# Down projection on one Trainium2 core: the sample rows' weight tiles taken in three turns instead of six in the first half of d_model

## What is computed

```python
def swiglu(h, w_gate, w_up, w_down):
    return (jax.nn.silu(h @ w_gate) * (h @ w_up)) @ w_down
...
        yp = yp + swiglu(rms_norm(yp, g_ffn[l]), w_gate[l], w_up[l], w_down[l])
        ys = ys + swiglu(rms_norm(ys, g_ffn[l]), w_gate[l], w_up[l], w_down[l])
```

## Time and profile before

| | before |
|---|---|
| median of three runs | 1028.95 us |
| the profiled execution | 1032.31 us |
| its span, first to last instruction | 1030.6 us |
| mean granted TensorE clock | 0.999 |
| TensorE busy | 1006.1 us, 98% of the span |
| VectorE, ScalarE, GpSimd busy | 61%, 38%, 40% |
| line 1482 (sample's tiles) | 88 records, 818.8 to 955.2 us |

### The profile page before, as it was taken

How to read it: one execution, slowest core, us unless ns; L and a number is a source line. 1 busy time by engine, 2 the same in 40 slices (tenths; PEclk the granted TensorE clock), 3 DMA queues, 4 the chain that set the end, 5 groups by cost and what they waited for, 6 DMA issues and landing times.

```text
span 1030.6 us, 16280 instructions
## 1 busy us (share of the span) xinstructions
PE 1006.1 (98%) x5754; PEld 836.8 (81%) x5754; DVE 625.8 (61%) x877; ACT 389.1 (38%) x701; POOL 408.4 (40%) x444
## 2 busy tenths in 40 slices
PE   5999999999999999999999999999999999999997
PEld 4999998888887787787787787877878776877786
DVE  5476637766245696676667567666754737634725
ACT  5411235445233443333333334333333446334431
POOL 2001100000000367697696787876964400201045
PEclk9999999999999999999999999999999999999999
DMA  8311331100321444553643643644637999578814
GB/s 277 96 51 43 84 85 43 43 2 1 123 103 67 148 113 130 160 165 109 190 151 113 193 144 112 201 135 134 184 110 227 296 335 385 188 281 310 308 41 169
DMA packets 166274, 155.84 MB, mean 151 GB/s; under 512 B 16240, under 2 KB 129296, under 8 KB 166224
## 3 DMA queue, kind: packets, MB, share of 16 engines
q1 hardware_dynamic: 166224, 155.16, 46.8%
HBM read 114.17 MB, written 41.06 MB: 151 GB/s over the span
## 4 chain that ended last, share of the span: by engine, by line
PE 84%; DMA 7%; DVE 4%; SPq 1%; issue 1%; ACT 1%; POOL 1%; POOLq 0%; ACTq 0%; DVEq 0%
PE ps L1108 26%; PE ps L1110 25%; PE ps L1109 25%; DMA xd_in<-act_scratch 2%; PE ps L1394 2%; PE ps L1145 1%; PE ps L1280 1%; DMA act_scratch<-act_sums 1%; DMA y_acc_odd<-in_w_down 1%; PE ps L1258 1%; DMA out_state_gmlp_v_sample<-work 1%; DMA act_scratch<-ffn_blocks_odd 1%; PE ps L1482 1%; PE ps L1242 1%; DMA act_scratch<-ffn_blocks_even 1%
## 5 line engine op out<-in xcount | busy, mean ns | idle before, releaser
L1108 PE MATMUL ps<-x_forms,w_forms 128*128 128x512 f32 (+1 forms) x644 | 246.4, 383 | 2.0 <-DVE w_forms L1903 1.7
L1109 PE MATMUL ps<-x_forms,w_forms 128*128 128x512 f32 (+1 forms) x644 | 244.7, 380 | 0.0
L1110 PE MATMUL ps<-x_forms,w_forms 128*128 128x512 f32 (+1 forms) x644 | 244.5, 380 | 0.0
L1108 PEld LDWEIGHTS ps<-x_forms,w_forms 128*128 128x128 f32 x644 | 121.0, 188 | 29.9 <-issue 4.8
L1110 PEld LDWEIGHTS ps<-x_forms,w_forms 128*128 128x128 f32 x644 | 121.1, 188 | 23.0
L1109 PEld LDWEIGHTS ps<-x_forms,w_forms 128*128 128x128 f32 x644 | 121.1, 188 | 22.4
L1108 PE MATMUL ps<-w_dn,x_dn 128*128 128x512 f32 x308 | 121.5, 394 | 0.0
L1110 PE MATMUL ps<-w_dn,x_dn 128*128 128x512 f32 x308 | 120.0, 390 | 0.0
L1109 PE MATMUL ps<-w_dn,x_dn 128*128 128x512 f32 x308 | 119.9, 389 | 0.0
L955 POOL TENSOR_SCALAR meansq<-sumsq 128x1 f32<-128x1 f32 (+1 forms) x26 | 9.8, 376 | 249.2 <-ACT xn_ffn L1530 224.1
L1689 ACT CAST w_forms<-w_sums 128x512 fp32r<-128x512 f32 x88 | 54.6, 623 | 111.1 <-PE ps L1110 108.7
(11 more groups left out here) (254 smaller groups left out, 2113.2 us busy)
## 6 DMA issues: line engine op xcount, KB each, us to landing
xd_in<-act_scratch SPq DMA_DIRECT2D x35, 512.0 KB, 7.3
t_raw<-in_w_down SPq DMA_DIRECT2D x88, 128.0 KB, 2.5
act_scratch<-act_sums SPq DMA_DIRECT2D x22, 512.0 KB, 4.1
y_acc_odd<-in_w_down SPq DMA_DIRECT2D x22, 512.0 KB, 6.3
wd_in<-t_scratch SPq DMA_DIRECT2D x20, 512.0 KB, 6.9
wd_in<-in_w_down SPq DMA_DIRECT2D x15, 512.0 KB, 6.7
stage<-in_w_in SPq DMA_DIRECT2D x28, 256.0 KB, 3.6
w_stage_even<-in_w_gate SPq DMA_DIRECT2D x22, 256.0 KB, 3.3
```

The lines of the kernel that those rows point to most:

```text
L1108: mm(out, wh, xh, start=first, stop=False, skip_group_check=onto)
L1109: mm(out, wh, xl, start=False, stop=False, skip_group_check=onto)
L1110: return mm(out, wl, xh, start=False, stop=last, skip_group_check=onto)
```

## The change

The six turns of the first half, with 2, 2, 2, 2, 2 and 1 tiles, become three with 4, 4 and 3. The loads of tiles 6 and 7 are issued two groups earlier in the queue. Tiles 8, 9 and 10, which were issued ahead of k = 14 (two) and k = 16 (one), are issued together ahead of k = 13. The second half is as it was.

```diff
-SAMPLE_TURNS = {(0, 3): 2, (0, 5): 2, (1, 1): 2, (1, 2): 2, (1, 3): 2, (1, 4): 1,
+SAMPLE_TURNS = {(0, 5): 4, (1, 2): 4, (1, 4): 3,
                 (3, 0): 2, (3, 2): 2, (3, 4): 2, (4, 0): 2, (4, 2): 2, (4, 3): 1}
 EARLY_SLOTS, LATE_SLOTS = 4, 2
 
-RAW_LOADS = {(1, 2): range(4, 6), (1, 5): range(6, 8), (2, 2): range(8, 10), (2, 4): range(10, 11),
+RAW_LOADS = {(1, 2): range(4, 6), (1, 3): range(6, 8), (2, 1): range(8, 11),
              (3, 5): range(11, 13), (4, 1): range(13, 15), (4, 3): range(15, 17), (5, 0): range(17, 19),
              (5, 2): range(19, 21), (5, 4): range(21, 22)}
```

## The result

| | before | changed |
|---|---|---|
| median | 1028.70 us (6 runs, 1027.25 to 1030.61) | 1033.08 us (6 runs, 1032.45 to 1033.86) |
| ratio | | 1.0034, 95% interval 1.0023 to 1.0045 |
| profiled execution, span | 1032.31, 1030.6 us | 1032.97, 1031.3 us |
| mean granted TensorE clock | 0.999 | 0.995 |

By the ratio the changed kernel is slower by 0.34%, 3.5 us with 2.4 to 4.6 as its interval; the two medians of the table are 4.4 us apart, inside that interval. The forecast was no change (1028.8 us), and its range ended at 1030.9. The granted clock was 0.995 in all six timed runs as well.

The account below looks back on a forecast made before the run. TensorE's chain and a full DMA queue were taken as bounds, meeting at row tile 3 of group 12. TensorE's 9.88 - 6.84 = 3.04 us gain mostly became a 2.9 us wait: 1028.95 - 0.1 = 1028.8 us, range 1026.6 to 1030.9.

Parts of the forecast that it names:

- The cost of a turn: On TensorE, a turn of two tiles costs 1.20 us, one of three or four tiles 2.08 us.
- the sum: On TensorE, 9.88 us removed less 6.84 added: 3.04 us early after turn (1, 4), of which 0.1 us is left.
- The removed waits: TensorE's waits for tiles at turns (1, 3) and (1, 4), 2.56 and 0.12 us, go.
- The new wait for x8: TensorE reaches group 8 earlier and waits 0.6 us for the low part of x8.
- The gain goes into a wait for the adds at row tile 3 of group 12: TensorE arrives there at 867.90 and waits 2.9 us for VectorE's sample adds, ending at 870.76.
- "The same bytes stand ahead of x16 in both kernels, so if the DMA queue never runs dry, x16 lands where it did": In the DMA queue, x16 isn't delayed by the reordered loads; its cast starts again near 865.7 us.
- The third rival: The DMA queue runs dry while SP stands at tiles 8 to 10; x16 lands late, 1030.9 us; chance 0.10.
- "[...] by the rows, 1028.8, since the gap is still shorter than the one that was followed by a fall": At row tile 3, a 2.9 us wait keeps TensorE's clock full; the fall seen followed more than 3.4 us idle.
- The price of a fall: A clock fall at row tile 3's wait would cost about 1.6 us, from 3.5 us at half clock.
- the second rival: TensorE's clock falls to half in the new wait at row tile 3: 1028.8 + 1.6 = 1030.4 us; chance 0.10.

Follow-up runs that it names:

- tile_3_later: Changed kernel with row tile 3 of group 12 moved on TensorE behind row tile 2 of group 13; 1027.89 us, ratio 0.9976 to the kernel before.
- adds_earlier_2: Changed kernel with VectorE's four sample adds moved ahead of the low parts of groups 15 and 16; 1027.07 us, ratio 0.9977 to the kernel before.
- after_look_2: Second profile of the changed kernel, without an edit; span 1031.8 us.
- loads_later: Changed kernel with tiles 6 and 7 issued ahead of group 10 instead of group 9; 1031.50 us, ratio 1.0016 to the kernel before.
- turns_alone: Kernel before with the new three turns (SAMPLE_TURNS) and the old RAW_LOADS; 1031.32 us, ratio 1.0015 to the kernel before.
- loads_alone: Kernel before with the old six turns (SAMPLE_TURNS) and the new RAW_LOADS; 1030.67 us, ratio 1.0011 to the kernel before.
- adds_later_1: Kernel before with VectorE's four sample adds moved behind the low parts of group 17; 1031.27 us, ratio 1.0009 to the kernel before.

## Why the prediction was wrong

- **The cost of a turn** (1.20 and 2.08 us): right, 2.06 measured, and 1.1 us for merging in the profiles where the sum has 0.96.
- **The removed waits** (2.68 us): too large as a typical value. The other two profiles have 2.0 and 1.1 us. I noted that the profiled execution lay 3.36 us over the median and still carried its waits over. It didn't harm the sum, since in every profile of the kernel before row tile 3 follows the adds by about 0.2 us, whatever tile 10 did; but I took that for chance.
- **The new wait for x8** (0.6 us): didn't come. TensorE lost 0.1 us at group 8 in the first profile of the change and nothing in the second. It only made the next wait longer.
- **The gain goes into a wait for the adds at row tile 3 of group 12**: right, in its place, its releaser and its cause; tile_3_later and adds_earlier_2 show it from two sides. Its size was off: 4.0 and 3.2 us where 2.9 was expected.
- **"The same bytes stand ahead of x16 in both kernels, so if the DMA queue never runs dry, x16 lands where it did"**: the condition didn't hold. The third rival had the place in part. In the first profile of the change SP issues x11 at 837.22 and w12 at 841.23, 4.0 us later, since w9 stood behind tiles 6 and 7 and its low part came late; ahead of tile 8 it waits for tile 4's use, 1.2 us there and 1.6 in after_look_2, where it had also waited 1.3 us for earlier tiles. The start of x16's cast, counted from the first down matmul, spreads by 1.6 us over the three profiles of the kernel before, which is more than the 0.8 us in question. All profiles with the old and all with the new `RAW_LOADS` (seven and eight, loads_later apart) have means of 68.3 and 69.1 us, 0.8 apart again, with spreads of 3.0 and 2.0. How the 0.8 us divide among these causes stays open.
- **"[...] by the rows, 1028.8, since the gap is still shorter than the one that was followed by a fall"** is the step that failed. I compared the expected 2.9 us with the one idle stretch that was followed by a fall and gave the fall one chance in ten. In all six timed runs of the change the mean clock was 0.995. turns_alone then showed a fall behind 2.50 us of waiting. The earlier trace rows proved only that a long wait is enough, not that a shorter one is safe. The Trainium skill, "TensorE: Matmul & The Clock Gate", section "Why this matters for your kernels", warns of idle gaps between bursts of matmuls. The traces agree: 3.96 and 3.19 us were both followed by half clock.
- **The price of a fall** (1.6 us) was too low: 2.9 us in the profiles. I priced 3.5 us at half clock, from the start of the program; here it was 6.8 us, of which 1.2 passed in the wait in the first profile. In the other 5.6 us there was time for 13 matmuls, 0.43 us apart instead of 0.227 (the first took 0.60).

So the second rival happened, 1.3 us dearer than it was priced, on top of a part of the third. At its measured price it alone leaves the range: 1028.8 + 2.9 = 1031.7, over 1030.9.

## What to carry to other kernels

A stage that is freed on one engine arrives early somewhere: look for its next semaphore, and in which order the releasing engine gets there. If a gain becomes a wait of some microseconds on TensorE, it can cost more than it brought, since matmuls behind it may run at half clock; so move the releaser, or work that needs no release, into the gap before merging anything. Here the change with the adds moved (0.9977 of the kernel before) and the change with row tile 3 moved (0.9976) are the best versions that were run.

## What was not expected of the hardware

The clock's fall can't be read from the length of one wait. Waits of TensorE in the down projection and what followed, one profile each: 0.58, 0.92, 1.15, 1.60 and 1.95 us, clock full; 2.50 us, half for 3.4 us; 3.19, 3.96 and 6.35 us, half for 6.8 us each. Yet a shorter one can do it elsewhere. At the start of the feed-forward block every profile has a wait of TensorE for a low part, 1.39 to 1.74 us long. In 3 of the 16 profiles (loads_alone, adds_later_1, tile_3_later) the clock was at half for 3.4 us behind it. These three have the longest wait, 1.74 us, but turns_alone has it too, and there the clock stayed full, as it did in the four profiles with 1.73. The timeline and busy times of loads_alone, then those of turns_alone:

```profile
352.12 0.28 PE L1110 MATMUL ps<-x_forms,w_forms 128*128 128x256 f32 x1
354.14 0.39 PE L1108 MATMUL ps<-x_forms,w_forms 128*128 128x256 f32 x1 [1.74 <-DVE w_forms L1903]
...
355.57 0.41 PE L1108 MATMUL ps<-x_forms,w_forms 128*128 128x256 f32 x1
```

```profile
355.60:359.00 3.40, 3.40 (x20) 3.40 (x20) 2.09 (x4) 1.43 (x3) 2.02 (x2) 0.59 0.18 53
```

```profile
354.36 0.39 PE L1108 MATMUL ps<-x_forms,w_forms 128*128 128x256 f32 x1 [1.74 <-DVE w_forms L1903]
```

```profile
355.60:359.00 3.40, 3.40 (x31) 3.40 (x31) 3.40 (x6) 2.59 (x4) 1.80 (x2) 1.00 0.25 80
```

So a wait of 1.74 us was followed by a fall in three profiles and not in a fourth, and each of the three waits over 3 us by one. Falls of this kind can add to the scatter between runs of one kernel; how much was not measured.

The profile of loads_later has a full clock behind the wait for the adds and takes 232.8 us from the first down matmul to the end, against 233.6 as the mean of the kernel before; yet in timed runs it is 1.6 us slower. The clocks of its other runs, 0.995 to 0.997, point to falls that this one execution was spared. For loads_alone, 233.4 us in its profile and 1.1 us slower in timed runs, they hardly do: seven of its twelve runs stand at 0.999 and three at 0.998. Part of its gap may be that the profiled executions of the kernel before were slower than its typical ones. Where the 1.1 us go was not shown.

Landings of the same loads move between executions of the same kernel, though the instructions ahead are the same: in the three profiles of the kernel before w9's cast starts 41.5 to 43.3 us and x16's 67.85 to 69.49 us behind the first down matmul. A stretch bound by the DMA queue needs more than one profile.
